# A hybrid decoder step on one core: each gate and up weight set loaded as two column halves

## The chip, the cores and the metric

One core of one Trainium2 chip. The metric is the device time of one execution in microseconds, here the median of three executions; lower is better. TensorE is called PE, VectorE DVE, ScalarE ACT, GpSimd POOL and SyncE SP.

## The reference, cut to what matters

One layer runs on 2048 prompt rows and 64 sample rows of width 1024. Attention and an mLSTM come first; the change is in the feed-forward part behind them:

```python
x = x + jnp.concatenate([o_att, o_ml], axis=-1) @ w_out
h2 = rms_norm(x, norm_ffn_w)
g, u = jnp.split(h2 @ w_ffn_in, 2, axis=-1)            # 1024 -> 2 x 2816
gc = conv_b + gp[:, 0:T] * conv_w[0] + gp[:, 1:T + 1] * conv_w[1] + gp[:, 2:T + 2] * conv_w[2]
x = x + (jax.nn.silu(gc) * u) @ w_down                 # 2816 -> 1024
```

`gp` is `g` with the last two rows of before in front. All of it is float32.

## The kernel before, in words

The function `late` holds the output projection (17 positions of up to 128 rows) and the whole feed-forward part. Three groups of rows go through the feed-forward part one after another: group 0 has 512 prompt rows and the 64 sample rows (576 columns in a tile, H = 288), groups 1 and 2 have 768 prompt rows each (H = 384). The 2816 columns of the feed-forward layer are cut into NP = 11 pieces of 256, so a group has 11 steps, 33 in all. A step `r = (G, i)` does on PE:

- unit 0, the gate columns of piece i: seven block products (a Strassen-Winograd scheme on 2 x 2 blocks of rows of the weights and columns), each of 12 matmuls, since every float32 factor is split into a rounded high part and a low part and three of the four products are formed;
- the down projection of the step before, 10 items of 6 matmuls in group 0 and 12 in groups 1 and 2, into four PSUM banks in turn; an item waits until DVE has added the one four items back (`added`);
- unit 1, the up columns of piece i: seven block products again.

The semaphore `prod` counts block products, 14 a step. In the last step of a group only 4 down items (SPLIT) stand between the two units.

A weight set is 1024 rows x 256 columns, 1 MB. Buffer `b_raw[0]` takes the gate sets and `b_raw[1]` the up sets; each is used anew at every step. In `b_raw[u]` the 128 columns x = 0 serve the block products n = 0 and n = 2 (`B11`, `B21`) and the columns x = 1 the products n = 4 and n = 6 (`T1`, `B22`); products 1, 3 and 5 read three sums (T2, T3, T4) that lie in `t_raw[u]`. The low parts lie in the place of the raw ones. A set goes through these hands:

1. SP issues the load: `load_up(r)` when all 14 products of the step before are done, `load_gate(r)` when the first 7 products of the step before are (L2017 to L2023, issued in L2015). Its order is up(i), gate(i+1), then the down weights of step i (`load_d`, L2030), which waits for the last down item.
2. POOL forms four sums one after another, `sums_b` (L2649, L2651, L2653, L2655), each 128 x 512. The first reads x = 1 only, the second overwrites the x = 1 block.
3. ACT rounds four pieces (`round_b`, L2292), DVE subtracts (`split_b`, L2466); piece q = 0 is x = 0, pieces 1 and 2 are the sums, piece 3 is x = 1. Every `split_b` waits for the fourth sum.

DVE's queue in a step, in the order of the code (`step`): the low parts of the activations and of the down weights (`split_act` L2476, `split_d` L2471), `combine` 0 of unit 0 (L2494, adds a PSUM bank into `gp`), combines 1 to 3, `split_b` of the up set q = 0, combine 4, then **the taps**: `tap(r, 0)`, the first `add` of the down items (L2520), `tap(r, 1)`, adds 1 to 3, `split_b` q = 1, adds and splits in turn. A tap is the two scalar-times-tensor additions of the convolution (L2506, and L2509 for the sample rows in group 0). POOL's queue: `gate` x = 0 and 1 (L2663, silu(gc) * u of the step before), `heads`, the four sums of the up set, `tails`, the four sums of the next gate set.

```python
            def load_up(r):
                w_prod(sp, before(r), 13)
                load_b(1, r[1])
...
                tap(r, 0)
                add(p, 0)
                tap(r, 1)
```

Of the kernel before, what the change touches and what calls it, by code (L numbers as in the profile page):

```python
# [23 lines left out]
P = 128  # L24
D = 1024
KC = D // P
# [9 lines left out]
FF = 2816  # L36
# [1712 lines left out]
NP = FC // 2  # L1749
# [17 lines left out]
def late(nc, ident, mhalf, ins, outs, o_dram, x1_dram, h2_dram, conv_cols, halo):  # L1767
# [14 lines left out]
    with ExitStack() as ctx:  # L1782
        k = Stage(nc, ctx, "late")
# [10 lines left out]
        def twin(name, at, shape):  # L1794
            return put(f"{name}_raw", at, shape), put(f"{name}_lo", at, shape, F32R)
# [24 lines left out]
        b_raw, b_lo = zip(twin("b0", at_b0, [P, SET // 4]), twin("b1", at_b1 + 20 * D, [P, SET // 4]))  # L1820
# [27 lines left out]

        acc_in, y_out = ([k.sem(f"{n}{j}") for j in range(ntile)] for n in ("acc_in", "y_out"))
        d_in, b_in, a_in = k.sem("d_in"), [k.sem("b_in0"), k.sem("b_in1")], [k.sem(f"a_in{n}") for n in range(4)]  # L1850
        a_summed, a_rounded, a_split = (k.sem(n) for n in ("a_summed", "a_rounded", "a_split"))
        b_summed, b_rounded, b_split = k.sem("b_summed"), k.sem("b_rounded"), k.sem("b_split")
        d_rounded, d_split = k.sem("d_rounded"), k.sem("d_split")
# [7 lines left out]
        def at(sem, per):  # L1861

            def w(eng, r, s):
                if r is not None:
                    eng.wait_ge(sem, per * (r[0].index * NP + r[1]) + s + 1)
            return w

        w_prod, w_cact, w_cdve = at(prod, 14), at(c_act, 4), at(c_dve, 10)
# [6 lines left out]
        def before(r):  # L1875

            G, i = r
            return (G, i - 1) if i else (groups[G.index - 1], NP - 1) if G.index else None
# [28 lines left out]
        def A_raw(slot, G):  # L1907
            return a_slot(a_raw, slot, G, A_TAIL // 4)
# [73 lines left out]
        def _(sp):  # L1982
            def load_o(p):
                o_turned.wait(sp, p - 2)
                o_in.mark(sp.dma_start(o[0:p.rows, p.p, :], o_dram[p.row:p.row + p.rows, :]), p)

            def load_x(p):
                x1_out.wait(sp, p - 2)
                src = ins["x_sample"].rearrange("b t d -> (b t) d") if p.sample else ins["x_prompt"][0, p.row:p.row + P, :]
                x_in.mark(sp.dma_start(x1[0:p.rows, p.p, :], src), p)  # L1990

            def store_x1(p):
                x_normed.wait(sp, p)
                x1_out.mark(sp.dma_start(x1_dram[p.tile, 0:p.rows, :], x1[0:p.rows, p.p, :]), p)

            def store_h(p):
                h_kept.wait(sp, p)
                sp.dma_start(h2_dram[:, 0, :, p.row:p.row + P], h_t[:, :].rearrange("p (c r) -> p c r", r=P)).then_inc(h_out, 16)
# [11 lines left out]
                    wait(sp, y_out[j], 16 * sum(g.ntile > j for g in groups[:G.index]))  # L2010
                sp.dma_start(acc[0:r, j, :], x1_dram[G.tile(j), 0:r, :]).then_inc(acc_in[j], 16)

            def load_b(u, i):
                src = ins["w_ffn_in"][0].rearrange("(c p) n -> p c n", p=P)[:, :, i * 2 * P + u * FF:i * 2 * P + u * FF + 2 * P]
                sp.dma_start(b_raw[u][:, :].rearrange("p (c n) -> p c n", c=KC), src).then_inc(b_in[u], 16)  # L2015

            def load_up(r):  # L2017
                w_prod(sp, before(r), 13)
                load_b(1, r[1])

            def load_gate(r):
                w_prod(sp, before(r), 6)
                load_b(0, r[1])  # L2023

            def load_d(r):
                if r == LAST:
# [33 lines left out]
            for p in positions:  # L2060
                if p.c >= 1:
                    store_x1(p - 1)
                    if p.c < LAST_AT:
                        load_x(p + 1)
                if p.c + 2 <= LAST_AT:
                    load_o(p + 2)
                if p.c - 2 > SAMPLE_AT:
                    store_h(p - 2)
                if p.c == SAMPLE_AT + 1:
                    load_b(0, 0)  # L2070
                if p is final:
                    proj.wait(sp, p - 1)
                    load_b(1, 0)
            proj.wait(sp, final)
            load_d(FIRST)
            for j in range(groups[0].ntile):
# [551 lines left out]
        @block.gpsimd  # L2628
        def _(pool):
            def rstd_x(p):  # L2630
                x_normed.wait(pool, p - 1)
                x_var.wait(pool, p)
                x_rstd.mark(nc.gpsimd.tensor_tensor(xr[0:p.rows, :], xvar[0:p.rows, :], mhalf[0:p.rows, 0:1], ALU.pow))

            def first_a(n):

                G = groups[0]
                out, x, y, op = A_SUMS[n]
                h_kept.wait(pool, positions[SAMPLE_AT])
                wait(pool, a_summed, n)  # L2640
                nc.gpsimd.tensor_tensor(A_raw(out, G), A_raw(x, G), A_raw(y, G), op).then_inc(a_summed, 1)

            def sums_b(r, u):
                if r is None:
                    return
                pool.wait_ge(b_in[u], 16 * (r[0].index * NP + r[1] + 1))
                b = lambda part, x: b_part(b_raw[u], part, x)
                tt = lambda n: t_raw[u][:, (n - T2) * KH * P:(n - T2 + 1) * KH * P].rearrange("p (c n) -> p c n", c=KH)
                nc.gpsimd.tensor_tensor(tt(T3), b(1, 1), b(0, 1), ALU.subtract).then_inc(b_summed, 1)  # L2649
                w_summed(pool, r, 4 * u)  # L2650
                nc.gpsimd.tensor_tensor(b(0, 1), b(0, 1), b(0, 0), ALU.subtract).then_inc(b_summed, 1)  # L2651
                w_summed(pool, r, 4 * u + 1)
                nc.gpsimd.tensor_tensor(tt(T2), b(1, 1), b(0, 1), ALU.subtract).then_inc(b_summed, 1)  # L2653
                w_summed(pool, r, 4 * u + 2)
                nc.gpsimd.tensor_tensor(tt(T4), b(1, 0), tt(T2), ALU.subtract).then_inc(b_summed, 1)  # L2655

            def gate(r, x):
                G = r[0]
                w_silu(pool, r, x)
                if x == 0:  # L2660
                    w_cact(pool, r, 3)
                w_cdve(pool, r, 5 + 3 + x)
                nc.gpsimd.tensor_tensor(t[:, x, 0:G.TG], t[:, x, 0:G.TG], whole(G, x), ALU.mult).then_inc(act_made, 1)  # L2663

            def heads(r):
                G, i = r
                w_made(pool, before(r), 1)
                nc.gpsimd.tensor_copy(cc[:, :, :], conv_cols[:, 2 * i * CC:2 * (i + 1) * CC].rearrange("p (x c) -> p x c", x=2)).then_inc(cols_kept, 1)
                if G.index == 0:
                    ins_ = nc.gpsimd.memset(gp[:, :, 0:HEAD], 0.0)  # L2670
                else:
                    ins_ = nc.gpsimd.tensor_copy(gp[:, :, 0:HEAD], halo[:, 2 * i * HEAD:2 * (i + 1) * HEAD].rearrange("p (x c) -> p x c", x=2))
                if G.sample:
                    w_cols(pool, r, 0)
                    ins_ = nc.gpsimd.tensor_copy(gs[:, :, :, 0:HEAD], cc[:, :, 0:NSC].rearrange("p x (b c) -> p x b c", b=SB))
                ins_.then_inc(head_kept, 1)

            def tails(r):
                G, i = r
                w_cdve(pool, r, 3)  # L2680
                if G.sample:
                    mine = gp[:, :, HEAD + G.pn:HEAD + G.TG].rearrange("p x (b t) -> p x b t", b=SB)
                    nc.gpsimd.tensor_copy(gs[:, :, :, HEAD:], mine)
                    nc.gpsimd.tensor_copy(conv_s[:, 2 * i * NSC:2 * (i + 1) * NSC].rearrange("p (x b c) -> p x b c", x=2, b=SB),
                                          mine[:, :, :, ST - HEAD:ST])
                w_head(pool, r, 0)
                nc.gpsimd.tensor_copy(halo[:, 2 * i * HEAD:2 * (i + 1) * HEAD].rearrange("p (x c) -> p x c", x=2),
                                      gp[:, :, G.pn:G.pn + HEAD]).then_inc(tail_kept, 1)

            def step(r):  # L2690
                G, i = r
                p = before(r)
                if p is not None:
                    gate(p, 0)
                    gate(p, 1)
                heads(r)
                sums_b(r, 1)
                tails(r)
                sums_b(after(r), 0)

            for p in positions:
                rstd_x(p)
                if 6 <= p.c < 8:
                    first_a(2 * (p.c - 6))
                    first_a(2 * (p.c - 6) + 1)
                if p.c == 9:
                    sums_b(FIRST, 0)
            proj.wait(pool, final)
            pool.wait_ge(cols_laid, 1)
            for G in groups:  # L2710
                for i in range(NP):
                    step((G, i))
            gate(LAST, 0)
            gate(LAST, 1)
# [79 lines left out]
```

## Time and profile before

| | |
|---|---|
| median of 3 executions | 2603.99 us (2601.41 to 2605.61) |
| the profiled execution | 2600.42 us |
| its span, first to last instruction | 2598.7 us |
| mean granted TensorE clock | 0.961 |
| busy share of the span | PE 93%, DVE 63%, ACT 35%, POOL 34% |
| loads of a weight set | 66 of 1 MB, median 5.1 us from issue to landing |
| POOL's wait for these loads | 193.2 us in 59 waits |

The feed-forward part runs from about 1115 us to the end. Rows of a timeline give the start, the duration, the engine and line, the operation and, in brackets, how long the engine was idle before it and who ended that. A row with "x2" merges two neighbours of one kind; for SPq its duration runs from the first issue to the end of the last. The rows of windows give for each engine its busy us and the instructions, then the granted clock, the mean busy share of the 16 DMA engines and what they moved in GB/s.

### The profile page before, as it was taken

The page shows a single profiled execution, that of the slowest core. Times are in us where ns is not written, and L with a number is a line of the kernel's source. Part 1 is how long each engine was busy: PE and PEld are TensorE (multiplying, and loading weights), DVE is VectorE, ACT ScalarE, POOL GpSimd, SP SyncE. Part 2 cuts the span into 40 slices and gives each one's busy share as a digit, 9 for nine tenths or more (in the row PEclk, how much of TensorE's full clock was granted, in tenths as well). Part 3 has the DMA queues.
Part 4 walks back from the last instruction along what each step waited for, and adds up shares of the span by engine and source line. Part 5 has one row for each costly group of instructions (what it writes and reads, how often), then busy time and mean ns, then how long its engine had stood idle before and what let it go on. Part 6 is the DMA issues. An engine that isn't in the chain of part 4 may idle for free.

```text
span 2598.7 us, 36568 instructions
## 1 busy us (share of the span) xinstructions
PE 2420.8 (93%) x13782; PEld 2198.9 (85%) x13782; DVE 1637.2 (63%) x2481; ACT 906.2 (35%) x1556; POOL 875.0 (34%) x700
## 2 busy tenths in 40 slices
PE   5999977999997699979999979999999899999999
PEld 4888866999996477778888878999999789999998
DVE  3666661666666433457776777676676876666766
ACT  2444441333332222234333343333333433333332
POOL 2223310221221003044554434344544443445432
PEclk9999977999997799989999989999999999999999
DMA  7222102111110434442222234221122341221121
GB/s 279 86 98 99 73 24 69 60 56 61 44 49 14 160 126 130 151 147 96 82 82 86 93 98 153 69 78 65 65 65 82 97 162 65 82 66 65 65 77 70
DMA packets 140404, 233.35 MB, mean 90 GB/s; under 512 B 17329, under 2 KB 105101, under 8 KB 138205
## 3 DMA queue, kind: packets, MB, share of 16 engines
q1 hardware_dynamic: 139953, 231.42, 26.5%
q8 instruction: 88, 1.44, 0.2%
q14 instruction: 43, 0.35, 0.0%
q10 hardware_dynamic: 288, 0.07, 0.0%
q0 software_dynamic: 32, 0.07, 0.0%
HBM read 180.36 MB, written 52.12 MB: 89 GB/s over the span
## 4 chain that ended last, share of the span: by engine, by line
PE 54%; DVE 4%; DMA 3%; issue 2%; POOL 1%; ACT 1%; SPq 0%; POOLq 0%; ACTq 0%; DVEq 0%
PE late_bank L2185 10%; PE late_bank L2186 10%; PE late_bank L2187 10%; PE late_bank L109 8%; PE late_bank L111 8%; PE late_bank L110 8%; DMA h_parts<-late_h_t 2%; DMA late_b_raw<-in_w_ffn_in_dram 1%; DVE late_act_lo L2476 1%; POOL late_t L2663 1%; DVE late_t_lo L2466 1%; DMA x<-late_x 1%; DVE late_hn L2438 0%; DMA late_a_raw<-h_parts 0%; DVE late_gp L2494 0%
## 5 line engine op out<-in xcount | busy, mean ns | idle before, releaser
L2494 DVE TENSOR_TENSOR late_gp<-late_bank,late_gp 128x384 f32<-128x384 f32 (+1 forms) x330 | 172.6, 523 | 335.0 <-PE late_bank L2187 333.7
L2185 PE MATMUL late_bank<-late_a_hi,late_b_hi 128*128 128x384 f32 (+1 forms) x1056 | 344.3, 326 | 14.4 <-ACT late_gp L2324 7.0
L2186 PE MATMUL late_bank<-late_a_lo,late_b_hi 128*128 128x384 f32 (+1 forms) x1056 | 343.0, 325 | 0.0
L2187 PE MATMUL late_bank<-late_a_hi,late_b_lo 128*128 128x384 f32 (+1 forms) x1056 | 341.9, 324 | 0.0
L2663 POOL TENSOR_TENSOR late_t<-late_t,late_gp 128x768 f32<-128x768 f32 (+1 forms) x66 | 129.5, 1980 | 520.3 <-DVE late_gp L2494 520.3
L109 PE MATMUL late_bank<-late_d_hi,late_act_hi 128*128 128x512 f32 (+1 forms) x724 | 285.8, 395 | 15.1 <-DVE late_acc L2520 9.1
L111 PE MATMUL late_bank<-late_d_hi,late_act_lo 128*128 128x512 f32 (+1 forms) x724 | 284.7, 393 | 0.0
L110 PE MATMUL late_bank<-late_d_lo,late_act_hi 128*128 128x512 f32 (+1 forms) x724 | 284.5, 393 | 0.0
L2185 PE MATMUL late_bank<-late_a_hi,late_t_hi 128*128 128x384 f32 (+1 forms) x792 | 261.3, 330 | 18.3 <-DVE late_gp L2494 9.2
L2520 DVE TENSOR_TENSOR late_acc<-late_bank,late_acc 128x512 f32<-128x512 f32 (+1 forms) x374 | 243.9, 681 | 39.6 <-PE late_bank L111 38.9
L2186 PE MATMUL late_bank<-late_a_lo,late_t_hi 128*128 128x384 f32 (+1 forms) x792 | 257.4, 325 | 0.0
L2187 PE MATMUL late_bank<-late_a_hi,late_t_lo 128*128 128x384 f32 (+1 forms) x792 | 256.6, 324 | 0.0
L2324 ACT ACTIVATE late_gp<-late_bank 128x384 f32<-128x384 f32 (+1 forms) x132 | 61.3, 465 | 508.1 <-PE late_bank L2187 508.1
L2185 PEld LDWEIGHTS late_bank<-late_a_hi,late_b_hi 128*128 128x128 f32 x1056 | 200.0, 189 | 17.4 <-issue 9.4
L109 PE MATMUL ml_bank<-att_next_hi,ml_hh 128*128 128x386 f32 (+1 forms) x544 | 194.6, 358 | 14.8 <-DMA ml_hh<-h_parts 14.8
L2186 PEld LDWEIGHTS late_bank<-late_a_lo,late_b_hi 128*128 128x128 f32 x1056 | 200.1, 189 | 1.6
L2187 PEld LDWEIGHTS late_bank<-late_a_hi,late_b_lo 128*128 128x128 f32 x1056 | 200.1, 189 | 0.0
L111 PE MATMUL ml_bank<-att_next_hi,ml_hh 128*128 128x386 f32 (+1 forms) x544 | 187.9, 345 | 0.0
L110 PE MATMUL ml_bank<-ahead_ml_w_lo,ml_hh 128*128 128x386 f32 (+1 forms) x544 | 187.6, 345 | 0.0
L109 PEld LDWEIGHTS late_bank<-late_d_hi,late_act_hi 128*128 128x128 f32 (+1 forms) x724 | 134.9, 186 | 47.9 <-DVE late_acc L2520 12.4
L2185 PEld LDWEIGHTS late_bank<-late_a_hi,late_t_hi 128*128 128x128 f32 x792 | 150.2, 190 | 27.1 <-issue 19.8
L2466 DVE TENSOR_TENSOR late_b_lo<-late_b_raw,late_b_hi 128x1024 fp32r<-128x1024 f32 x132 | 162.1, 1228 | 12.2 <-ACT late_b_hi L2292 6.3
(326 smaller groups left out, 5417.0 us busy)
## 6 DMA issues: line engine op xcount, KB each, us to landing
late_b_raw<-in_w_ffn_in_dram SPq DMA_DIRECT2D x66, 1024.0 KB, 5.1
late_d_raw<-in_w_down_dram SPq DMA_DIRECT2D x32, 1024.0 KB, 4.8
ml_hh<-h_parts SPq DMA_DIRECT2D x16, 1024.0 KB, 4.8
att_x<-in_x_prompt_dram SPq DMA_DIRECT2D x16, 512.0 KB, 3.7
h_parts<-att_h_hi SPq DMA_DIRECT2D x16, 512.0 KB, 2.7
h_parts<-att_h_lo SPq DMA_DIRECT2D x16, 512.0 KB, 3.4
late_o<-mixed SPq DMA_DIRECT2D x16, 512.0 KB, 5.2
late_x<-in_x_prompt_dram SPq DMA_DIRECT2D x16, 512.0 KB, 4.0
```

The source lines that it names most:

```text
L109: nc.tensor.matmul(out, a_hi, b_hi, start=first, stop=False)
L110: nc.tensor.matmul(out, a_hi, b_lo, start=False, stop=False)
L111: return nc.tensor.matmul(out, a_lo, b_hi, start=False, stop=last)
L2185: nc.tensor.matmul(out, w_h, hi[:, c, :], start=first, stop=False, skip_group_check=True)
L2186: nc.tensor.matmul(out, w_h, lo[:, c, :], start=False, stop=False, skip_group_check=True)
L2187: ins_ = nc.tensor.matmul(out, w_l, hi[:, c, :], start=False, stop=last, skip_group_check=True)
L2324: nc.scalar.activation(dst, bank[0][:, 0:G.H], ACT.Copy).then_inc(c_act, 1)
L2466: nc.vector.tensor_tensor(lo, raw, hi.bitcast(F32), ALU.subtract).then_inc(b_split, 1)
L2476: nc.vector.tensor_tensor(act_lo[:, x, lo:hi], t[:, x, lo:hi], act_hi[:, x, lo:hi].bitcast(F32), ALU.subtract).then_inc(act_split, 1)
L2494: nc.vector.tensor_tensor(dst, bk, src, ALU.add).then_inc(c_dve, 1)
L2520: nc.vector.tensor_tensor(sl, bank[8 - RING + N % RING][0:rows, :], sl, ALU.add).then_inc(added, 1)
L2663: nc.gpsimd.tensor_tensor(t[:, x, 0:G.TG], t[:, x, 0:G.TG], whole(G, x), ALU.mult).then_inc(act_made, 1)
```

## The change

A set is no longer loaded by one DMA of 256 columns but by two of 128 columns, x = 0 and x = 1. The half x = 0 waits only for the block product n = 2 of its unit, the last that reads these columns, the half x = 1 waits for n = 6 as the whole set did. A second pair of semaphores `b2_in` counts the halves x = 1. ACT's rounding of piece q = 0 still waits for `b_in` alone, which now stands for the half x = 0; POOL's sums wait for both. For the first two sets of all both halves are issued together.

```diff
+        b2_in = [k.sem("b2_in0"), k.sem("b2_in1")]
...
-            def load_b(u, i):
-                src = ins["w_ffn_in"][0].rearrange("(c p) n -> p c n", p=P)[:, :, i * 2 * P + u * FF:i * 2 * P + u * FF + 2 * P]
-                sp.dma_start(b_raw[u][:, :].rearrange("p (c n) -> p c n", c=KC), src).then_inc(b_in[u], 16)
+            def load_b(u, i, x):
+                at_ = i * 2 * P + u * FF + x * P
+                src = ins["w_ffn_in"][0].rearrange("(c p) n -> p c n", p=P)[:, :, at_:at_ + P]
+                sp.dma_start(b_raw[u][:, :].rearrange("p (c n) -> p c n", c=KC)[:, :, x * P:(x + 1) * P], src).then_inc((b_in, b2_in)[x][u], 16)
 
             def load_up(r):
+                w_prod(sp, before(r), 9)
+                load_b(1, r[1], 0)
                 w_prod(sp, before(r), 13)
-                load_b(1, r[1])
+                load_b(1, r[1], 1)
 
             def load_gate(r):
+                w_prod(sp, before(r), 2)
+                load_b(0, r[1], 0)
                 w_prod(sp, before(r), 6)
-                load_b(0, r[1])
+                load_b(0, r[1], 1)
...
             def sums_b(r, u):
                 if r is None:
                     return
+                pool.wait_ge(b2_in[u], 16 * (r[0].index * NP + r[1] + 1))
                 pool.wait_ge(b_in[u], 16 * (r[0].index * NP + r[1] + 1))
```

The order on SP, before the steps begin (the last store of the normed rows, `h_parts<-late_h_t`) and in the first steps of group 0. Before:

```order
L2015 DMA late_b_raw<-in_w_ffn_in_dram 128x8x256
L2030 DMA late_d_raw<-in_w_down_dram 128x2x1024
L2011 DMA late_acc<-x 128x1024 x4
L2011 DMA late_acc<-x 64x1024
L1998 DMA h_parts<-late_h_t 128x8x128
L1994 DMA x<-late_x_4783 128x1024
L1998 DMA h_parts<-late_h_t 128x8x128
L2015 DMA late_b_raw<-in_w_ffn_in_dram 128x8x256 x3
L2030 DMA late_d_raw<-in_w_down_dram 128x2x1024
L2015 DMA late_b_raw<-in_w_ffn_in_dram 128x8x256 x2
L2030 DMA late_d_raw<-in_w_down_dram 128x2x1024
```

And with the change:

```order
L2017 DMA late_b_raw<-in_w_ffn_in_dram 128x8x128 x2
L2036 DMA late_d_raw<-in_w_down_dram 128x2x1024
L2012 DMA late_acc<-x 128x1024 x4
L2012 DMA late_acc<-x 64x1024
L1999 DMA h_parts<-late_h_t 128x8x128
L1995 DMA x<-late_x_4783 128x1024
L1999 DMA h_parts<-late_h_t 128x8x128
L2017 DMA late_b_raw<-in_w_ffn_in_dram 128x8x128 x6
L2036 DMA late_d_raw<-in_w_down_dram 128x2x1024
L2017 DMA late_b_raw<-in_w_ffn_in_dram 128x8x128 x4
L2036 DMA late_d_raw<-in_w_down_dram 128x2x1024
```

Nothing changes its place on SP; each load of a set is two, in the order up x = 0, up x = 1, gate x = 0, gate x = 1. The instructions of PE, ACT, DVE and POOL keep their order too; only POOL's first sum of each set waits for a second semaphore.

## Rows read from the trace of the kernel before

**Rows 1.** The page: shares of the chain that ended last, by engine
```profile
PE 54%; DVE 4%; DMA 3%; issue 2%; POOL 1%; ACT 1%; SPq 0%; POOLq 0%; ACTq 0%; DVEq 0%
```

**Rows 2.** Timeline of PE: matmuls before which it sat idle, feed-forward part
```profile
1308.60 0.37 PE L2185 MATMUL late_bank<-late_a_hi,late_t_hi 128*128 128x288 f32 x1 [0.71 <-DVE late_gp L2494]
1396.43 0.50 PE L109 MATMUL late_bank<-late_d_hi,late_act_hi 128*128 128x512 f32 x1 [0.57 <-DVE late_acc L2520]
1513.11 0.61 PE L2185 MATMUL late_bank<-late_a_hi,late_t_hi 128*128 128x288 f32 x1 [4.41 <-DVE late_t_lo L2466]
2032.39 0.45 PE L2185 MATMUL late_bank<-late_a_hi,late_t_hi 128*128 128x384 f32 x1 [1.01 <-DVE late_t_lo L2466]
```

**Rows 3.** Timeline of SP: each row an up set's issue and a gate set's
```profile
1340.19 12.40 SPq L2015 DMA_DIRECT2D late_b_raw<-in_w_ffn_in_dram  x2
1377.06 12.40 SPq L2015 DMA_DIRECT2D late_b_raw<-in_w_ffn_in_dram  x2
1414.80 12.50 SPq L2015 DMA_DIRECT2D late_b_raw<-in_w_ffn_in_dram  x2
1489.57 12.48 SPq L2015 DMA_DIRECT2D late_b_raw<-in_w_ffn_in_dram  x2
1687.04 15.43 SPq L2015 DMA_DIRECT2D late_b_raw<-in_w_ffn_in_dram  x2
```

**Rows 4.** Timeline of POOL: first sum of a set (up, gate; last up; gate)
```profile
1382.23 2.38 POOL L2649 TENSOR_TENSOR late_t_raw<-late_b_raw 128x512 f32<-128x512 f32 x1 [0.87 <-DMA late_b_raw<-in_w_ffn_in_dram]
1394.11 1.59 POOL L2649 TENSOR_TENSOR late_t_raw<-late_b_raw 128x512 f32<-128x512 f32 x1 [3.88 <-DMA late_b_raw<-in_w_ffn_in_dram]
1496.54 1.30 POOL L2649 TENSOR_TENSOR late_t_raw<-late_b_raw 128x512 f32<-128x512 f32 x1 [2.67 <-DMA late_b_raw<-in_w_ffn_in_dram]
1707.14 1.30 POOL L2649 TENSOR_TENSOR late_t_raw<-late_b_raw 128x512 f32<-128x512 f32 x1 [5.43 <-DMA late_b_raw<-in_w_ffn_in_dram]
```

**Rows 5.** Timeline of DVE: a step of group 0 from 1388, of group 1 from 1705
```profile
1388.75 1.28 DVE L2466 TENSOR_TENSOR late_b_lo<-late_b_raw,late_b_hi 128x1024 fp32r<-128x1024 f32 x1 [0.77 <-POOL late_t_raw L2655]
...
1392.81 0.74 DVE L2506 SCALAR_TENSOR_TENSOR late_t<-late_gp,late_cc,late_t 128x512 f32<-128x512 f32 x1
1393.47 0.28 DVE L2509 SCALAR_TENSOR_TENSOR late_t<-late_gs,late_cc,late_t 128x64 f32<-128x64 f32 x1
1393.79 0.75 DVE L2506 SCALAR_TENSOR_TENSOR late_t<-late_gp,late_cc,late_t 128x512 f32<-128x512 f32 x1
1394.46 1.32 DVE L2509 SCALAR_TENSOR_TENSOR late_t<-late_gs,late_cc,late_t 128x64 f32<-128x64 f32 x1
1395.70 1.88 DVE L2520 TENSOR_TENSOR late_acc<-late_bank,late_acc 128x512 f32<-128x512 f32 x3
...
1705.16 2.06 DVE L2506 SCALAR_TENSOR_TENSOR late_t<-late_gp,late_cc,late_t 128x768 f32<-128x768 f32 x2
1707.14 1.88 DVE L2520 TENSOR_TENSOR late_acc<-late_bank,late_acc 128x512 f32<-128x512 f32 x3
```

**Rows 6.** Timeline of DVE in the last step of group 0: the up set's sums
```profile
1511.61 2.58 DVE L2466 TENSOR_TENSOR late_t_lo<-late_t_raw,late_t_hi 128x512 fp32r<-128x512 f32 x2
```

**Rows 7.** Windows: a set's load; cache loads in 512-byte pieces; `late_h_t`'s store in 512-byte pieces
```profile
1379.50:1380.00 0.50, 0.50 (x6) 0.50 (x5) 0.50 (x1) 0.45 (x1) 0.44 (x2) 1.00 1.10 391
19.00:20.00 1.00, 0.00 (x0) 0.00 (x0) 0.81 (x2) 1.00 (x2) 0.10 (x1) 1.00 1.21 289
1132.50:1133.00 0.50, 0.00 (x0) 0.00 (x0) 0.50 (x1) 0.50 (x2) 0.00 (x0) 0.50 0.99 288
```

**Rows 8.** By tile: issues of `late_b_raw` and their landing; landing of `late_h_t`, 512 KB
```profile
L2015 SPq DMA_DIRECT2D late_b_raw<-in_w_ffn_in_dram x66: 367/368/1041, 957.0 to 2530.3; - x66
DMA to landing us min/median/max: 4.8/5.1/8.5
DMA to landing us min/median/max: 3.5/6.3/13.4
```

**Rows 9.** The chain that ended last: `late_h_t`'s store before the first steps
```profile
1116.57 13.37 DMA h_parts<-late_h_t
```

More of the change, by code:

```diff
@@ L2069, in _ @@
                 if p.c == SAMPLE_AT + 1:
-                    load_b(0, 0)
+                    load_b(0, 0, 0)
+                    load_b(0, 0, 1)
                 if p is final:
                     proj.wait(sp, p - 1)
-                    load_b(1, 0)
+                    load_b(1, 0, 0)
+                    load_b(1, 0, 1)
             proj.wait(sp, final)
```

## The prediction

> **What bounds the kernel now.** I read the page first: PE is busy for 93% of the span, and over half of the chain that ended last is PE's [rows 1]. So a load is worth only what PE waits for because of it. Next PE's timeline, for the rows before which it sat idle [rows 2]. In group 0 there is a wait of 0.71 us in each of ten steps, for the first combine, behind POOL's gates and the low parts of the activations; no load is in it. Two steps have 0.57 and 0.50 us more before the sixth down item, behind DVE's adds. The last step of group 0 has 4.41 us before the up unit's second product, that of group 1 has 1.01 us. In all other steps of groups 1 and 2 PE never waits. POOL's 193 us of waiting for these loads are thus mostly idle time that costs nothing.
>
> Then the way of a set. SP issues it [rows 3], and POOL's first sum starts 5.17 us (up, 1382.23 - 1377.06) or 5.02 us (gate, 1394.11 - 1389.09, the second issue being the row's end less 0.37) behind the issue, in group 1 5.04 us (1707.14 - 1702.10) [rows 3, 4, 8]. I call the gate set's distance T. Last, what stands beside it on DVE [rows 5]. A sum and a DVE operation on two SBUF operands exclude each other: the sum that came at 1394.11 waited until the tap in progress was through (1.59 us in place of 1.30), and the next tap, L2509, waited for the sum: 1.32 us, where its twin at 1393.47 took 0.28. The adds read PSUM and are not held up: three take 1.88 us in either group. **In groups 1 and 2 the last tap ends at the very moment at which the gate set's first sum starts**, 1707.14. A sum that comes sooner meets a tap.
>
> **The price of a meeting.** Add 1 stands right behind the taps, and PE needs it for down item 5. PE comes there 6.77 us after the gate set's issue (1396.43 - 0.57 - 1389.09) [rows 2, 3]; items are of one length, so in groups 1 and 2 too. In group 1 add 1 now starts 5.04 us after the issue and takes 0.68 (an add's row where it stands alone is a third of 1.88 and a little more), so 1.0 us are to spare. One meeting pushes a tap by 1.0 to 1.3 us and costs 0 to 0.4; I take 0.35 a step. In group 0 the step hit at 1394.46 is 37.74 us long (1414.80 - 1377.06) and its neighbour that isn't is 36.87 (1377.06 - 1340.19) [rows 3]: 0.87 us, part of it because its taps stood late already.
>
> **The change, part by part.**
>
> *T.* A half is 512 KB in pieces of 512 bytes, a set now 1 MB in pieces of 1 KB. A set's load runs at 391 GB/s in mid-flight; loads of 512-byte pieces at the start of the kernel run at 289, a store of such pieces at 288 [rows 7]. 1049 KB at 391 GB/s is 2.68 us, 524 KB at 290 is 1.81: T falls by 0.9, to **4.1 to 4.2 us**. Bounds: if the number of pieces set the time, 1024 in either, T stays 5.0; the least of the store's landings, 512 KB in 512-byte pieces, is 3.5 [rows 8]. I take 4.15, since the rates are those of this piece size; the second wait of POOL costs at most the 0.1 us between two sums.
> The Trainium skill speaks against me here: DMA: Bandwidth & Descriptors, Specifications, gives 512 B as the least size at line rate. By that a half would run at the set's own rate, and T be 3.7: that is rival B, and the sum +16.9. This case's rows of 512-byte pieces, 288 and 289 GB/s, disagree with it.
>
> *Gate sets in group 0, nine steps.* The taps x = 1 start 3.72 and 4.70 us after the issue in the step shown, behind a `split_b` that waited 0.77 us for the up set's fourth sum [rows 5]; without that wait they stand some 0.65 us sooner, the second at about 4.05. With T = 4.15 the sum comes while this tap runs and pushes only the last small one, by 1.0 us: add 1 ends at about 6.8 in place of 5.8, PE waits 0.2. Nine steps, +1.8.
> *Up sets in group 0.* POOL is free 0.87 us before the load lands now [rows 4], so the sums gain at most that, and the wait of 0.77 us on DVE goes. The two steps of 37.7 us become ordinary: -1.7. The 0.71 us a step stay, as their chain has no load in it. What is late next is the tap chain above.
> *The last step of group 0.* Its up set's first sum starts 6.97 us after the issue (1496.54 - 1489.57), 1.8 later than others. Smaller and sooner, it starts at about 5: the fourth sum, the taps, the adds and `split_b` q = 1 follow some 1.3 us sooner. That `split_b` also stood behind the gate set's last sum (2.58 us for two that take 1.8 alone) [rows 6], which comes sooner as well: 1.0. Together -2.3 of the 4.41 us; bounds 0 (the delay of 1.8 us has another cause and stays) and -3.
> *Groups 1 and 2.* The second tap x = 1 starts 4.05 us after the issue (1705.16 + 1.0 - 1702.10). With T above that nothing is pushed, and PE has no wait to lose: 0.
> *The start.* The set issued at 1110.90 shares the queue with the store of `late_h_t` issued at 1116.57, which lands 13.37 us later and is on the chain that ended last [rows 9]. 1049 KB at 290 in place of 391 GB/s is +0.9 us for it; the gate set behind it lands later too and meets one tap fewer (-0.35 to -0.5). +0.4; bounds 0 and +1.5.
> *No price.* 66 more issues of 0.37 us [rows 8] on SP, which waits for PE before all of them. The half x = 0 waits for product 2, then SP stands before product 6 as it did, so nothing behind it (down weights, `load_next_a`) is issued later; DMA is idle when it comes. That half comes 5 us and more before it is needed, but only ACT's piece q = 0 could use it, and DVE takes that piece only behind the fourth sum. At the turn of a group both halves of the up set go out together behind the A loads: up to +0.5 us of landing, beside 3 us waits for A; I take 0, bounds -1 and +1.
>
> Sum: 0.4 + 1.8 - 1.7 - 2.3 = **-1.8 us**. The profiled execution took 2600.42, so 2598.6; the median shown is 3.57 higher, so **2602.2**.
>
> **The rivals.**
> *A: the sum pushes a tap in groups 1 and 2 as well* (T from 3.9 to 4.05). For it: T needs to be only 0.1 less than I take. Against: the rates. 18 steps of 0.35 = 6.3; the last step of group 1, where `split_b` stands behind the adds, +1.2. With -1.8 that is +5.7: **2609.7**.
> *B: the sum comes between the taps* (T under 3.9): it gets in ahead of the second large tap in group 0, the next sum gets in before the last tap, and add 1 ends 2.3 us later than now. PE waits 1.3 us in each of nine steps, 11.7, less the 1.7; the last step of group 0 gains only 1; groups 1 and 2 cost 7.5, the start 0.4: +16.9, **2620.9**. **This is the slower side; it decides from T = 3.9 down.** For it: the least landing of 3.5; against it, the two rates. The Trainium skill (DMA: Bandwidth & Descriptors, Anatomy of one DMA) estimates a load on POOL's queue at 2.0 us and the bytes over 436e3, 3.2 us for a half, deeper in this case still; for a whole set that gives 4.4, where the rows have 5.0.
> *C: the number of pieces, not their bytes, sets the time* (T over 4.5): nothing is pushed. -1.7 - 2.3 + 0.4, with the up sets gaining less: -2 to -5, **2600**. For it: a set of 1 KB pieces has as many as a half. Against: 289 GB/s at 512 bytes and 391 at 1 KB are not a factor of two.
> *D: nothing reaches PE.* The gains fail and so do the pushes: 2604.
>
> **How the numbers follow.** My case (T 4.05 to 4.5) 0.42, A 0.20, B 0.20, C 0.10, D 0.08. The likeliest gives 2602. A measurement of this kernel tells 0.2%, 5.2 us, from no change. Faster needs C at its best, or my case with the turns of the groups gaining: 0.12. Slower is B and most of A, which lies at that bound: 0.35. The rest, 0.53, is the same. The range leaves out B's full price and goes from C's best end, 2598, to the room between A and B, 2617.
>
> **What would show it.** In the profile after: landings of a half, median 3.9 to 4.2 us; POOL's first gate sum about 4.15 us after the second issue; in group 0 a small tap L2509 of about 1.3 us in every step and a PE wait of some 0.2 us before the sixth down item; in groups 1 and 2 two taps still 2.06 us for two and PE without a wait; the 4.41 us down to about 2. Wrong if the down items wait in groups 1 and 2 (A), if large taps of 1.7 to 2 us stand in group 0 (B), if landings stay at 5 us (C), or if the last step of group 0 keeps its 4.4 us.

## The result, and the profile after

The changed kernel is slower: 2617.76 us median of 5 executions (2614.3 to 2618.36), before 2603.99 (2597.7 to 2605.61, 5 executions); ratio 1.0055, 95% interval 1.004 to 1.007. The forecast was 2602, its range ended at 2617. The profiled executions are 2616.91 and 2600.42 us, 16.5 apart; spans 2615.2 and 2598.7, mean granted clock 0.961 in both.

The page of the changed kernel, shares of the chain that ended last by engine:

```profile
PE 50%; DVE 6%; POOL 4%; DMA 3%; issue 3%; ACT 1%; SPq 0%; POOLq 0%; DVEq 0%; ACTq 0%
```

PE has 4% less of the chain than before [rows 1], POOL 3% and DVE 2% more: something now runs through these two. Where it is, PE's timeline tells by its rows with idle time. Of the kernel before, five more such rows than stand above, as marks (the second block product of the first and of the tenth counted step of group 0, and the down items at the turns and the end):

```profile
1161.00 0.38 PE L2185 MATMUL late_bank<-late_a_hi,late_t_hi 128*128 128x288 f32 x1 [0.71 <-DVE late_gp L2494]
1494.98 0.37 PE L2185 MATMUL late_bank<-late_a_hi,late_t_hi 128*128 128x288 f32 x1 [0.71 <-DVE late_gp L2494]
1564.92 0.50 PE L109 MATMUL late_bank<-late_d_hi,late_act_hi 128*128 128x512 f32 x1 [2.92 <-DVE late_d_lo L2471]
2083.75 0.50 PE L109 MATMUL late_bank<-late_d_hi,late_act_hi 128*128 128x512 f32 x1 [2.92 <-DVE late_d_lo L2471]
2571.52 0.50 PE L109 MATMUL late_bank<-late_d_hi,late_act_hi 128*128 128x512 f32 x1 [0.39 <-DVE late_acc L2520]
```

The same view of the changed kernel (its lines stand 8 further down, so L2528 is the add, L2474 `split_b`, L2514 and L2517 the taps):

```profile
1161.42 0.37 PE L2193 MATMUL late_bank<-late_a_hi,late_t_hi 128*128 128x288 f32 x1 [0.71 <-DVE late_gp L2502]
...
1366.58 0.50 PE L109 MATMUL late_bank<-late_d_hi,late_act_hi 128*128 128x512 f32 x1 [1.00 <-DVE late_acc L2528]
...
1405.78 0.50 PE L109 MATMUL late_bank<-late_d_hi,late_act_hi 128*128 128x512 f32 x1 [2.03 <-DVE late_acc L2528]
...
1483.28 0.50 PE L109 MATMUL late_bank<-late_d_hi,late_act_hi 128*128 128x512 f32 x1 [2.08 <-DVE late_acc L2528]
...
1508.66 0.37 PE L2193 MATMUL late_bank<-late_a_hi,late_t_hi 128*128 128x288 f32 x1 [0.71 <-DVE late_gp L2502]
...
1526.12 0.61 PE L2193 MATMUL late_bank<-late_a_hi,late_t_hi 128*128 128x288 f32 x1 [3.81 <-DVE late_t_lo L2474]
...
1579.00 0.50 PE L109 MATMUL late_bank<-late_d_hi,late_act_hi 128*128 128x512 f32 x1 [2.92 <-DVE late_d_lo L2479]
...
2100.11 0.50 PE L109 MATMUL late_bank<-late_d_hi,late_act_hi 128*128 128x512 f32 x1 [2.92 <-DVE late_d_lo L2479]
...
2587.98 0.50 PE L109 MATMUL late_bank<-late_d_hi,late_act_hi 128*128 128x512 f32 x1 [0.39 <-DVE late_acc L2528]
```

From mark to mark, with the waiting product of the last step of group 0 [rows 2] between:

| stretch | before | after | difference |
|---|---|---|---|
| to the first mark | 1161.00 | 1161.42 | +0.4 |
| nine steps of group 0 | 333.98 | 347.24 | **+13.3** |
| last step of group 0, to its waiting product | 18.13 | 17.46 | -0.7 |
| turn to group 1 | 51.81 | 52.88 | +1.1 |
| group 1, with the turn to group 2 | 518.83 | 521.11 | +2.3 |
| group 2 | 487.77 | 487.87 | +0.1 |

The loss is in group 0. In eight of the nine steps PE now waits before the sixth down item, behind DVE's add 1: five times 0.8 to 1.0 us and three times 2.03 to 2.08. Before, two steps did, by 0.57 us [rows 2] and 0.50 (at 1434.22). These waits together are 10.7 us in place of 1.1. The rest of the 13.3 is that each step with a wait is 0.3 to 0.4 us longer than the wait explains (39.20 us with 2.03, where an ordinary step is 36.87; why, no run shows), and one stretch at a slower clock, for which see the end. What stands ahead of add 1 is seen on DVE and POOL. SP's row first, then POOL's sums, then DVE, for the step whose wait is 2.03 us. The second half of the gate set is the last of the row's three issues, at 1384.94 + 12.40 - 0.37 = 1396.97:

```profile
1384.94 12.40 SPq L2017 DMA_DIRECT2D late_b_raw<-in_w_ffn_in_dram  x3
```

```profile
1400.73 1.29 POOL L2658 TENSOR_TENSOR late_t_raw<-late_b_raw 128x512 f32<-128x512 f32 x1 [3.23 <-DMA late_b_raw<-in_w_ffn_in_dram]
1402.09 1.28 POOL L2660 TENSOR_TENSOR late_b_raw<-late_b_raw 128x512 f32<-128x512 f32 x1
1403.45 1.59 POOL L2662 TENSOR_TENSOR late_t_raw<-late_b_raw 128x512 f32<-128x512 f32 x1
```

```profile
1400.07 0.75 DVE L2514 SCALAR_TENSOR_TENSOR late_t<-late_gp,late_cc,late_t 128x512 f32<-128x512 f32 x1
1400.73 1.37 DVE L2517 SCALAR_TENSOR_TENSOR late_t<-late_gs,late_cc,late_t 128x64 f32<-128x64 f32 x1
1402.14 1.79 DVE L2514 SCALAR_TENSOR_TENSOR late_t<-late_gp,late_cc,late_t 128x512 f32<-128x512 f32 x1
1403.85 1.28 DVE L2517 SCALAR_TENSOR_TENSOR late_t<-late_gs,late_cc,late_t 128x64 f32<-128x64 f32 x1
1405.05 1.88 DVE L2528 TENSOR_TENSOR late_acc<-late_bank,late_acc 128x512 f32<-128x512 f32 x3
```

T, from the issue to POOL's first sum, is 3.76 us here. The sum gets in behind the first large tap. From then on sum and tap take turns: taps of 0.28, 0.75 and 0.28 us take 1.37, 1.79 and 1.28, and add 1 starts 8.08 us after the issue. In the kernel before it starts 5.1 to 5.3 us after it in the steps without a meeting and 6.6 in the two with one. PE stood ready 6.78 us after the issue (1405.78 - 2.03 - 1396.97), just where the prediction had it.

Over the nine steps and the last of group 0, T is 3.75 to 4.09 us nine times and 4.51 once. With T of 4.09 (1358.76 to 1362.85) the sum gets in one tap later, in the same instant as the second large tap:

```profile
1362.85 1.84 DVE L2514 SCALAR_TENSOR_TENSOR late_t<-late_gp,late_cc,late_t 128x512 f32<-128x512 f32 x1
1364.62 1.31 DVE L2517 SCALAR_TENSOR_TENSOR late_t<-late_gs,late_cc,late_t 128x64 f32<-128x64 f32 x1
1365.85 1.88 DVE L2528 TENSOR_TENSOR late_acc<-late_bank,late_acc 128x512 f32<-128x512 f32 x3
```

Two pushes, a wait of 1.00 us. Hundredths decide between two and three: the step with T = 3.82 (issued at 1474.41) meets the small tap first and PE waits 2.08 us, the one with 3.83 (1243.41) comes just behind that tap's start and PE waits 0.85. Only the step with T = 4.51 shows what the prediction forecast for all: one small tap pushed (the row at 1211.06 below), no listed wait of PE, 37.10 us.

```profile
1210.39 0.75 DVE L2514 SCALAR_TENSOR_TENSOR late_t<-late_gp,late_cc,late_t 128x512 f32<-128x512 f32 x1
1211.06 1.31 DVE L2517 SCALAR_TENSOR_TENSOR late_t<-late_gs,late_cc,late_t 128x64 f32<-128x64 f32 x1
```

In group 1 the gate set's second half is issued at 1716.63 and summed from 1720.34, T = 3.71; two taps take 2.98 us, 0.92 more than in [rows 5]:

```profile
1719.70 2.98 DVE L2514 SCALAR_TENSOR_TENSOR late_t<-late_gp,late_cc,late_t 128x768 f32<-128x768 f32 x2
1722.60 1.87 DVE L2528 TENSOR_TENSOR late_acc<-late_bank,late_acc 128x512 f32<-128x512 f32 x3
```

No wait of PE is listed there, yet up sets are issued 46.18 us apart (1693.26 and 1739.44), before 45.96 (1687.04 and 1733.00): 0.2 us a step. One step of the same group is a control inside this run: its gate set's second half, issued at 1948.00, is summed only from 1953.14, no tap is pushed, and its up sets are 45.95 us apart (1924.63 and 1970.58), while the steps beside it have 46.39 and 46.42.

Over the gate sets of all groups behind the first steps the median of T is 5.2 us before and 3.9 after: it fell by 1.3 us, and not by 0.9. Why? The windows of half a microsecond over a load in group 1 (busy us by engine, granted clock, share of the DMA engines, GB/s), a whole set before and then a half after:

```profile
1703.00:1703.50 0.50, 0.50 (x4) 0.38 (x4) 0.50 (x1) 0.50 (x1) 0.00 (x0) 1.00 0.30 66
1703.50:1704.00 0.50, 0.50 (x4) 0.42 (x3) 0.46 (x2) 0.50 (x2) 0.00 (x0) 1.00 0.73 229
1704.00:1704.50 0.50, 0.50 (x4) 0.42 (x3) 0.50 (x1) 0.50 (x2) 0.00 (x0) 1.00 1.06 379
...
1706.00:1706.50 0.50, 0.50 (x4) 0.42 (x3) 0.46 (x2) 0.50 (x2) 0.00 (x0) 1.00 0.87 275
```

```profile
1717.50:1718.00 0.50, 0.50 (x4) 0.42 (x3) 0.50 (x1) 0.50 (x1) 0.00 (x0) 1.00 0.39 109
1718.00:1718.50 0.50, 0.50 (x4) 0.39 (x3) 0.47 (x2) 0.50 (x2) 0.00 (x0) 1.00 1.04 309
1718.50:1719.00 0.50, 0.50 (x4) 0.42 (x3) 0.50 (x1) 0.50 (x2) 0.00 (x0) 1.00 1.05 305
1719.00:1719.50 0.50, 0.50 (x4) 0.42 (x3) 0.50 (x2) 0.50 (x1) 0.00 (x0) 1.00 0.91 272
1719.50:1720.00 0.50, 0.50 (x4) 0.42 (x3) 0.50 (x2) 0.50 (x2) 0.00 (x0) 1.00 0.18 53
```

The half runs at the rate that the prediction took from pieces of this size, some 300 GB/s. It was above all the whole set that was priced wrongly: its data move from about 1703.2 to 1706.45, 3.2 us, and not the 2.7 that its peak rate of 391 GB/s gives. The half's move from about 1717.7 to 1719.7, 2.0 us in place of 1.8. Landings by tile, changed kernel:

```profile
DMA to landing us min/median/max: 3.6/3.9/10.4
```

A half lands in 3.9 us where a set took 5.1 [rows 8], 1.2 us sooner.

### The profile page after: what moved, and what is told of

Read it like the earlier page. It is cut to its first block, busy times and chain, and to the rows that moved or that the text cites. A ratio compares the mean times of both kernels' runs of the same rounds, so it can differ in the third digit from the quotient of the medians.

```text
span 2615.2 us, 36700 instructions
## 1 busy us (share of the span) xinstructions
PE 2426.6 (93%) x13782; PEld 2197.2 (84%) x13782; DVE 1664.7 (64%) x2481; ACT 905.8 (35%) x1556; POOL 872.0 (33%) x700
## 3 DMA queue, kind: packets, MB, share of 16 engines
q8 instruction: 88, 1.44, 0.2%
## 4 chain that ended last, share of the span: by engine, by line
PE 50%; DVE 6%; POOL 4%; DMA 3%; issue 3%; ACT 1%; SPq 0%; POOLq 0%; DVEq 0%; ACTq 0%
PE late_bank L2193 10%; PE late_bank L2194 10%; PE late_bank L2195 9%; PE late_bank L109 7%; PE late_bank L110 7%; PE late_bank L111 7%; DMA h_parts<-late_h_t 2%; DVE late_t L2514 1%; DVE late_t L2517 1%; POOL late_t L2672 1%; DVE late_acc L2528 1%; POOL late_b_raw L2660 1%; POOL late_t_raw L2658 1%; DMA x<-late_x 0%; DVE late_t_lo L2474 0%
## 5 line engine op out<-in xcount | busy, mean ns | idle before, releaser
L2528 DVE TENSOR_TENSOR late_acc<-late_bank,late_acc 128x512 f32<-128x512 f32 (+1 forms) x374 | 242.9, 680 | 31.8 <-PE late_bank L111 31.5
L2474 DVE TENSOR_TENSOR late_b_lo<-late_b_raw,late_b_hi 128x1024 fp32r<-128x1024 f32 x132 | 161.0, 1220 | 8.7 <-ACT late_b_hi L2300 7.2
```

Source lines behind the costliest of these rows:

```text
L2474: nc.vector.tensor_tensor(lo, raw, hi.bitcast(F32), ALU.subtract).then_inc(b_split, 1)
L2528: nc.vector.tensor_tensor(sl, bank[8 - RING + N % RING][0:rows, :], sl, ALU.add).then_inc(added, 1)
```

## The experiments

P is the theory that the gate sums' place among the taps is the whole loss; Q that the halves or their pieces of 512 bytes cost something themselves. Ratios are to the kernel before, timed beside them.

| kernel | median us | ratio, 95% interval | nine steps of group 0 | wait in its last step |
|---|---|---|---|---|
| before | 2602.5 to 2604.0 | 1 | 334.0 | 4.41 |
| the change | 2617.76 | 1.0055 (1.004 to 1.007) | 347.2 | 3.81 |
| `hold` | 2595.53 | 0.9977 (0.9966 to 0.9989) | 332.2 | 1.35 |
| `up_halves` | 2596.82 | 0.9978 (0.9968 to 0.9989) | 332.3 | 0.50 |
| `gate_halves` | 2633.95 | 1.0123 (1.0104 to 1.0142) | 361.0 | 5.84 |
| `together` | 2599.8 | 0.9989 (0.9974 to 1.0004) | 333.6 | 3.38 |
| `late` | 2602.64 | 0.9995 (0.9981 to 1.0008) | 332.0 | 1.43 |
| `add_first` | 2615.98 | 1.0053 (1.0036 to 1.007) | 344.4 | 3.59 |
| `before_hold` | 2595.48 | 0.9972 (0.9957 to 0.9988) | 332.0 | 1.86 |
| `up_hold` | 2594.66 | 0.9968 (0.9954 to 0.9982) | 332.4 | 0.42 |
| `gate_hold` | 2595.78 | 0.9974 (0.9962 to 0.9986) | 332.4 | 1.98 |
| `hold_g0` | 2599.92 | 0.9999 (0.9986 to 1.0012) | 332.3 | 1.32 |

The fourth column is the distance of two rows of 0.71 us in PE's timeline, nine steps apart; the last column is PE's idle time before the up unit's second product in the last step. Both are of the profiled execution.

### Hold the gate sums back: `hold`

```diff
                 tails(r)
+                w_taps(pool, r, 3)
                 sums_b(after(r), 0)
```

> The changed kernel, but POOL's four sums of the gate set also wait for the step's last tap. Theory P (place in the queue): the loss comes only from the gate set's sums starting 3.7 us after the second half's issue instead of 5.0, so that they get in among DVE's taps and add 1 and down item 5 are late. Then no step of group 0 is longer than 36.9 us, the waits before the sixth down item are gone, groups 1 and 2 are back at 45.97 us a step, and the time is 2600 to 2603 us. Rival Q (traffic): loads in 512-byte pieces slow something else down (ACT, the low parts, PE's reads); then the waiting of POOL changes nothing or delays the low parts of the gate set, and the time stays at 2614 us or more.

Measured: 7.5 us faster than before (2602.98, timed beside it), 22 faster than the change, and 4.5 below the range that P had given. Loads, halves and pieces are those of the change, so Q falls. PE's rows, first and last mark of group 0 and the waiting product of its last step:

```profile
1160.24 0.38 PE L2193 MATMUL late_bank<-late_a_hi,late_t_hi 128*128 128x288 f32 x1 [0.71 <-DVE late_gp L2502]
...
1492.47 0.38 PE L2193 MATMUL late_bank<-late_a_hi,late_t_hi 128*128 128x288 f32 x1 [0.71 <-DVE late_gp L2502]
...
1507.43 0.40 PE L2193 MATMUL late_bank<-late_a_hi,late_t_hi 128*128 128x288 f32 x1 [1.35 <-DVE late_t_lo L2474]
```

Nine steps are 332.23 us, 36.9 each; the wait of 4.41 us in the last step has shrunk to 1.35, though a second one of 1.47 us, for the next combine, has come behind it. A third gain was not in P's sum. In the first step of all the gate set's sums and the taps met in the kernel before too, four of its eight taps took 1.28 to 1.77 us. ACT's silu, which stands ahead of its copy of the bank, waited for them, and PE for the copy, 6.63 us. With the hold that wait is 2.85:

```profile
1145.04 0.55 PE L2193 MATMUL late_bank<-late_a_hi,late_b_hi 128*128 128x288 f32 x1 [2.85 <-ACT late_gp L2332]
```

### One part alone: `up_halves` and `gate_halves`

In each one of the two loads is put back to the whole set at its old time. `up_halves`:

```diff
             def load_gate(r):
-                w_prod(sp, before(r), 2)
-                load_b(0, r[1], 0)
                 w_prod(sp, before(r), 6)
-                load_b(0, r[1], 1)
+                load_whole(0, r[1])
```

`gate_halves` has the same in `load_up` and keeps `load_gate`.

> Only the up sets are loaded as two halves, the gate sets whole at the old time. P: the gate set's first sum stays 5.0 us behind the issue and meets at most one tap, the up set's sums can start no sooner than POOL's gates let them: 2600 to 2604 us, the two steps of 37.7 us in group 0 gone or moved. Q: half of the 512-byte pieces, half of the loss: about 2610 us.

> Only the gate sets are loaded as two halves, the up sets whole at the old time. P: all of the loss is here: 2615 to 2620 us, nine steps of group 0 of 38 us and more, some 0.2 us more a step in groups 1 and 2. Q: half of the loss, about 2610 us.

The two parts have opposite signs: the up sets' halves gain 0.22%, the gate sets' lose 1.23%, more than the whole change, and neither P nor Q had that. The up set's halves move DVE's queue forward: `split_b` q = 0 stands ahead of the taps and waits for the up set's fourth sum. The last step of group 0 shows it. In `up_halves` no gate sum meets a tap there and PE waits 0.50 us:

```profile
1511.43 0.40 PE L2194 MATMUL late_bank<-late_a_hi,late_t_hi 128*128 128x288 f32 x1 [0.50 <-DVE late_t_lo L2475]
```

The product behind the second wait, of 1.47 us here too, starts 19.02 us after the step's mark, in the kernel before 23.46.

In `gate_halves` the up set comes late, the taps with it, and the gate set early. The gate set's second half is issued at 1409.01 and summed from 1412.95, T = 3.94; by that alone it should do as the milder steps of the change (T = 3.95, a wait of 0.90). But its tap x = 1 starts 3.41 us after the issue, in the change 3.10, and all three remaining taps are pushed:

```profile
1412.42 0.74 DVE L2515 SCALAR_TENSOR_TENSOR late_t<-late_gp,late_cc,late_t 128x512 f32<-128x512 f32 x1
1413.08 1.32 DVE L2518 SCALAR_TENSOR_TENSOR late_t<-late_gs,late_cc,late_t 128x64 f32<-128x64 f32 x1
1414.44 1.78 DVE L2515 SCALAR_TENSOR_TENSOR late_t<-late_gp,late_cc,late_t 128x512 f32<-128x512 f32 x1
1416.15 1.27 DVE L2518 SCALAR_TENSOR_TENSOR late_t<-late_gs,late_cc,late_t 128x64 f32<-128x64 f32 x1
```

So what decides is T less the taps' own start. In the change the two effects partly cancel. Five of the nine steps are 41.0 to 41.2 us long, though PE's waits in them are 2.25 to 2.59; the rest is the clock. PE's row after the wait, and a window behind it:

```profile
1418.08 0.79 PE L109 MATMUL late_bank<-late_d_hi,late_act_hi 128*128 128x512 f32 x1 [2.29 <-DVE late_acc L2529]
```

```profile
1418.00:1421.20 3.20, 3.12 (x7) 2.48 (x8) 2.58 (x6) 0.14 (x1) 0.70 (x1) 0.50 0.00 0
```

### The same loss, undone by the same line: `gate_hold`

`gate_halves` with the line of `hold`.

> Gate sets alone as halves (the slowest kernel so far, 2633.95 us), and POOL's gate sums wait for the last tap. P (the meetings are the whole of that loss): one wait on POOL takes away all of the 31 us: no step of group 0 over 37.0 us, 2595 to 2600 us, like the kernel before with the same wait (2595.48). Rival (part of the 31 us is the up set's whole load, in 1 MB beside halves, or SP's order): 2605 us or more stays.

One wait on POOL takes off 38 us and leaves 2595.78 us, the time of the kernel before with the same wait (`before_hold`, 2595.48). The meetings were the whole loss, and the falls of the clock inside the nine steps went with them.

### Halves at the old time: `together`

```diff
             def load_gate(r):
-                w_prod(sp, before(r), 2)
-                load_b(0, r[1], 0)
                 w_prod(sp, before(r), 6)
+                load_b(0, r[1], 0)
                 load_b(0, r[1], 1)
```

and so for `load_up`.

> All sets as two halves, but both halves issued together where the whole set was issued before. P: the second half lands behind the first, T is 5.0 us or more, and the loss is gone: 2602 to 2606 us. If 1 MB in 512-byte pieces runs at 290 GB/s, it lands about 0.9 us later than a whole set did, T about 6, which costs nothing since the sums then stand behind the taps. Q (512-byte pieces as such): 2615 us or more.

The time is 2 us below the range that P had given, and far from Q. The pieces are 512 bytes as in the change. SP issues four halves, the last two at 1702.71 and 1703.12:

```profile
1687.65 16.05 SPq L2017 DMA_DIRECT2D late_b_raw<-in_w_ffn_in_dram  x4
```

The same timeline in a window that holds the last issue alone:

```profile
1703.12 0.58 SPq L2017 DMA_DIRECT2D late_b_raw<-in_w_ffn_in_dram  x1
```

POOL's first sum is at 1708.48, 5.36 us behind the last issue and 5.77 behind the first, of which 0.41 are the second issue on SP. Whole sets have 5.04 in the step shown [rows 3, 4] and 5.2 in the median, so the smaller pieces cost some 0.2 us and did not make T shorter. It was the smaller number of bytes behind the last issue that did. One step of group 0 still has a meeting, a wait of 1.03 us.

### The gate half later: `late`

```diff
                 w_prod(sp, before(r), 6)
+                if before(r) is not None:
+                    w_down(sp, before(before(r)), 0)
                 load_b(0, r[1], 1)
```

> The changed kernel, but the second half of a gate set also waits for the first down item of the step (1.36 us behind block product 6). Pieces, halves and the up sets stay as in the change; only the time at which POOL's gate sums start moves back, to about 5.1 us behind product 6, as before. P (place in the queue): no tap is met, no wait before the sixth down item, steps of group 0 36.9 us, 2595 to 2599 us as with halves for the up sets alone. Q (something else in the gate set's halves): stays over 2610 us.

In the trace P holds: nine steps are 332.0 us, no wait before the sixth item, 1.43 us in the last step. The median is 3.6 us over P's range. The profiled execution shows where that lies: the third block product of its feed-forward part starts at 1128.16, that of before at 1117.96, and from there to the last down item it takes 1448.4 us where before takes 1453.6 (2571.52 - 1117.96). The first product is late already (1123.17, before 1114.21). Why the parts ahead, whose code is the same, took so much longer in this kernel is open; in all others the third product starts at 1118.0 to 1122.7.

### Add 1 ahead of the second tap pair: `add_first`

```diff
                     tap(r, 0)
                     add(p, 0)
+                    add(p, 1)
                     tap(r, 1)
                     n_adds = SPLIT if i == NP - 1 else p[0].NI
-                    for n in range(1, 8):
+                    for n in range(2, 8):
```

> The changed kernel, but DVE does add 1 ahead of the second tap pair (order tap 0, add 0, add 1, tap 1). The meetings of sums and taps stay, with taps of 1.2 to 1.8 us in the steps of group 0. P with add 1 as the path to PE: the waits before the sixth down item go or fall under 0.3 us, steps of group 0 36.9 to 37.2 us, 2596 to 2603 us; the last step of group 0 keeps 2 to 4 us of its wait. Rival (the meeting reaches PE by the low parts of the up set or by combine 0 of the up unit, which stand behind the taps too): waits appear before the up unit's products instead, and the time stays over 2608 us.

A miss, and neither side's reason: the wait moved one item on. PE comes to the seventh item 1.4 us after the sixth and needs add 2, which stands behind the taps:

```profile
1410.68 0.50 PE L109 MATMUL late_bank<-late_d_hi,late_act_hi 128*128 128x512 f32 x1 [1.22 <-DVE late_acc L2528]
```

Eight of nine steps are 38.4 us. In groups 1 and 2 a step is 45.97 us again (up sets issued at 1645.98 and 1691.95), so the 0.2 us there did come by add 1.

### The same wait in the kernel before, and with the up sets' halves: `before_hold`, `up_hold`

> The kernel before, with whole sets, but POOL's sums of the gate set also wait for the step's last tap. P: before too lost time by meetings in two steps of 37.7 us (1.7 us) and in the last step of group 0 (two taps of 1.67 and 1.28 us, 1.9 us of the 4.41 us wait): 0.9982 to 0.9990 of before, about 2599 us. Rival (the last step's wait is the up set's late landing alone): only 1.7 us, 0.9993.

> Only the up sets as halves, and POOL's gate sums wait for the last tap: no meeting is left. P: as with the up sets' halves alone, since there the taps were already through when the gate sums came: 2595 to 2598 us, 0.997 to 0.998 of before. A gain of more than 1 us over that would mean that meetings in groups 1 and 2 cost something there.

Both are as fast as `hold`: with the wait in place the halves, of one set or of both, bring nothing that the intervals can tell. P's size for `before_hold` was too small, in part by the first step of all, where PE's wait for the copy is 3.20 us in place of 6.63. The last step's wait is 1.86 us in `before_hold`, against 4.41: 2.55 us of it were meetings, the rest the late up set, which only the halves take away (0.42 in `up_hold`, with a second wait of 1.48 behind it).

### What groups 1 and 2 pay: `hold_g0`

> The changed kernel with the wait for the last tap in group 0 alone; in groups 1 and 2 the gate sums come as in the change. This prices the meetings of groups 1 and 2: by the steps of the change (46.18 us against 45.97) 0.2 us each, 17 to 18 steps, 3 to 4 us, so 2598 to 2600 us beside 2595.5 with the wait in all groups. If the 0.2 us have another cause they stay in both, and this run gives 2595 to 2597 us.

2599.92 us, as forecast and 4.4 over `hold`, though the intervals overlap by a little. The traces say it better: up sets 46.18 us apart here (1630.74 and 1676.92), 45.95 in `hold` (1628.01 and 1673.96).

## Why the prediction was wrong

**What bounds the kernel, and the mechanism: right.** In the nine steps PE waits behind add 1, add 1 behind the taps; sum and tap exclude each other, the waiting one gets in between two instructions. PE's arrival 6.77 us after the issue and the second large tap at 4.05 were right to 0.05 us (6.78; 4.09). In the one step with T over 4.15 the forecast fits too: 37.10 us, 0.23 over an ordinary one, where 0.2 was forecast.

**T: this step failed.** "1049 KB at 391 GB/s is 2.68 us, 524 KB at 290 is 1.81: T falls by 0.9" set a peak rate from mid-flight against the whole time of a load. The data of a set take 3.2 us, those of a half 2.0, so T fell by 1.3, to 3.75 to 4.09 in nine of ten steps of group 0 and to 3.70 to 4.18 in groups 1 and 2 but for one of 5.14. Two landings would have done better than two rates: the prediction had 5.1 us for 1 MB. The forecast also left no room: in groups 1 and 2 a T of 4.13 (issued at 1993.96) still pushed a tap and one of 4.18 (2146.40) did not, so that 4.15 lay on the edge itself. The windows here show 305 to 309 GB/s for pieces of 512 bytes against 379 to 389 for 1 KB. The Trainium skill (DMA: Bandwidth & Descriptors, Anatomy of one DMA) has a fit for POOL's queue; the estimate by it for the 512 KB that fall away is 1.2 us, and that is the difference measured (3.9 against 5.1), although its totals, 3.2 and 4.4, are 0.7 too small for these loads on SP's queue. The Trainium skill (DMA: Bandwidth & Descriptors, Specifications) gives 512 bytes as the least size at line rate; the rates of these windows disagree with it, and the T of 3.7 that the prediction drew from it came out near the measured 3.9 for another reason.

**Gate sets in group 0:** +1.8 forecast, and -1.7 for the two steps that become ordinary. The nine steps made +13.3. That is rival B, "the sum gets in ahead of the second large tap", whose chance was 0.20: it gave 11.7 - 1.7 = +10.0 for these steps. Its turning point, T of 3.9, was not right: up to 3.82 three taps are pushed and PE waits 2.0 to 2.1 us, from 3.83 to 4.09 two and it waits 0.8 to 1.0. Missing in it were the slower clock of one step, 1.8 us, and the 0.3 to 0.4 us by which a step grows beyond its wait. For the whole kernel B gave +16.9, and the profile has 16.5 (the medians 13.8). That they agree so well is luck: B was some 3 us too low here and priced groups 1 and 2 at 7.5, where 2.4 were measured.

**The last step of group 0:** -2.3 forecast, -0.7 measured. The 1.3 us for the up set's earlier sums were right: between `before_hold` and `up_hold` the wait falls by 1.44. The 1.0 us for gate sums that come sooner were not. The taps that these sums pushed made 2.55 us of the wait in the kernel before (`before_hold`), and coming sooner they pushed more of them.

**Groups 1 and 2:** 0 forecast, 0.2 us a step measured where rival A took 0.35. Group 1 lost 2.3. The prediction's "In all other steps of groups 1 and 2 PE never waits" passed over the turn between the two, where before has a wait of 4.09 us (at 2058.67). In group 2 nine steps lost 1.7 and the first won 1.6. Windows behind its start show that before ran there at a mean clock of 0.73 and the changed kernel at 1.00:

```profile
2085.00:2090.00 5.00, 5.00 (x17) 3.96 (x17) 4.39 (x5) 0.95 (x3) 4.01 (x3) 0.73 0.02 7
```

```profile
2101.00:2106.00 5.00, 5.00 (x24) 4.13 (x23) 4.95 (x5) 1.25 (x2) 4.74 (x3) 1.00 0.00 0
```

**The start and the issues:** +0.4 forecast, +0.4 measured at the first mark, but 0.3 of it was there at the feed-forward part's first product (1114.21 before, 1114.54 after), so the agreement is luck. No run shows a cost of the 66 more issues.

Two things were not weighed: that the two halves of the change work against each other through one queue, and that the loss could be taken off by an order, since POOL's gate sums can wait: `hold` delays them to 5.1 us behind the issue, and no step of group 0 gets longer by it.

## What to carry to other kernels

Data that come sooner start their consumer sooner; ask first what shares a port or a queue with it at that time, and whether anyone waits for its result. Here one semaphore wait that holds back work which is not urgent was worth at least as much as the faster load at its best (0.9972 of before with the wait alone, 0.9978 with the up sets' halves alone), and with the wait the halves added nothing that can be told from noise. Split a change that moves two loads and time the parts: one gained 0.2%, the other lost 1.2%. And price a shorter transfer by whole landings, not by the peak rate of one. Last, a forecast that rests on one instruction coming 0.1 us before or behind another should be given as two cases, and not as one number.

## What the runs showed that was not expected

- Short waits of PE can cost more than themselves. In the changed kernel a row of 2.08 us idle is followed by a stretch at the lower of the two clock levels (1.2 GHz):

```profile
1483.90:1487.10 3.20, 3.20 (x9) 2.46 (x8) 3.14 (x5) 0.00 (x0) 0.00 (x0) 0.51 0.03 5
```

  That step is 40.97 us long, its twin with 2.03 us idle and no fall 39.20. In `gate_halves` the clock fell behind waits of 2.25, 2.29, 2.35, 2.38 and 2.59 us and not behind 2.17 and 2.21 (the 3.8 us behind these are at 1.00), so the wait's length alone does not sort them.
- A two-operand DVE instruction of 0.28 us (64 columns) that meets a sum of 1.29 us loses as much as a large one, 1.0 us, and they alternate for as long as both queues have work. Adds that read PSUM are not touched (1.88 us for three, as before). The Trainium skill (SBUF — State Buffer, SBUF: two separate sides) describes such a lock, held for a whole instruction, and the meetings shown here agree.
- The peak rates of pieces of 512 bytes and of 1 KB differ by a fifth or more, yet it made little of a whole load: in `together` POOL's first sum starts 5.36 us behind the last issue of 1 MB in small pieces, and in nearly all steps 5.0 to 5.3 us behind that of a whole set.
